# Routing chain of a mixture-of-experts block: fewer steps per first maximum, the last tile's work reordered and partly on GpSimd

## What is computed

```
h = rmsnorm(x, norm2_g) * (1 + sc2) + sh2
g_sel = argmax(h @ w_group + b_group)                 # 1 of 4 groups
e_logits = (h @ w_expert + b_expert)[group g_sel]      # 8 experts of that group
top_v, top_i = top_k(e_logits, 2)
...
xb = rows of h that one expert got, in blocks of 128
ys = (silu(xb @ w1[e]) * (xb @ w3[e])) @ w2[e]
```

## Time and profile before

| what | value |
|---|---|
| median of 3 runs | 2083.99 us (2083.49 to 2084.51) |
| the profiled execution, its own time | 2083.16 us |
| its span on the core | 2080.8 us |
| busy share of the span | PE 96%, PEld 81%, DVE 66%, ACT 46%, POOL 8% |
| chain that ended last | PE 86%, DVE 4%, ACT 4%, issue 2%, DMA 2% |
| last matmul of the output projection begins | 1420.1 us of the span |
| first matmul of the first expert begins | 1447.9 us of the span |

### The profile page before, as it was taken

The page is one execution under the profiler, slowest core; times in us unless marked ns, Lnnn a source line. Parts: engine busy times, 40 slices in busy tenths (PEclk is TensorE's granted clock), DMA queues, the critical chain, the costliest instruction groups (busy, mean ns, idle before and its releaser), DMA issues.

```text
span 2080.8 us, 29320 instructions
## 1 busy us (share of the span) xinstructions
PE 2002.0 (96%) x10099; PEld 1677.0 (81%) x10099; DVE 1366.0 (66%) x2045; ACT 959.8 (46%) x1308; POOL 166.3 (8%) x114
## 2 busy tenths in 40 slices
PE   4999999999999999999999999997999999999995
PEld 4788888888888898888989888886788888888872
DVE  6545443112747658485674745567899999999986
ACT  5211111111453526436263444212888888888863
POOL 0000000000000000000000000000122222222210
PEclk6999999999999999999999999997999999999997
DMA  8142423222212112121120368645999999999955
GB/s 307 46 136 71 141 75 108 71 71 81 49 33 67 53 35 68 40 68 53 35 68 20 96 218 280 202 135 209 340 382 385 382 386 376 383 386 386 399 222 242
DMA packets 209398, 369.69 MB, mean 178 GB/s; under 512 B 43029, under 2 KB 155462, under 8 KB 183750
## 3 DMA queue, kind: packets, MB, share of 16 engines
q1 hardware_dynamic: 190614, 317.63, 43.8%
q10 hardware_dynamic: 9520, 34.63, 4.4%
q0 software_dynamic: 9216, 16.80, 2.1%
HBM read 336.96 MB, written 48.82 MB: 185 GB/s over the span
## 4 chain that ended last, share of the span: by engine, by line
PE 86%; DVE 4%; ACT 4%; issue 2%; DMA 2%; ACTq 1%; SPq 0%; DVEq 0%; POOLq 0%
PE ps L673 41%; PE ps L2581 16%; PE ps L2619 8%; PE ps L2481 4%; PE ps L2381 2%; PE ps L2348 2%; PE ps L2377 1%; PE ps L2567 1%; PE ps L2418 1%; PE ps L2388 1%; PE ps L2432 1%; PE ps L2331 1%; PE ps L2306 1%; PE ps L2603 1%; PE ps L2421 1%
## 5 line engine op out<-in xcount | busy, mean ns | idle before, releaser
L577 DVE TENSOR_TENSOR mw_lo<-mw_raw,mw_hi 128x2048 fp32r<-128x2048 f32 x192 | 436.9, 2289 | 48.9 <-ACT mw_hi L572 48.7
L673 PE MATMUL ps<-h_hi,w_lo 128*128 128x512 f32 x1152 | 463.9, 403 | 3.1 <-DVE h_lo L1453 2.3
L673 PE MATMUL ps<-h_hi,w_hi 128*128 128x512 f32 x1152 | 450.2, 391 | 0.0
L673 PE MATMUL ps<-h_lo,w_hi 128*128 128x512 f32 x1152 | 449.7, 390 | 0.0
L572 ACT ACTIVATE mw_hi<-mw_raw 128x2048 fp32r<-128x2048 f32 x192 | 368.2, 1919 | 117.0 <-PE ps L2581 67.2
L673 PEld LDWEIGHTS ps<-h_hi,w_hi 128*128 128x128 f32 x1152 | 216.9, 188 | 46.2
L673 PEld LDWEIGHTS ps<-h_hi,w_lo 128*128 128x128 f32 x1152 | 217.5, 189 | 43.7 <-issue 2.4
L673 PEld LDWEIGHTS ps<-h_lo,w_hi 128*128 128x128 f32 x1152 | 217.6, 189 | 39.0
L2581 PE MATMUL ps<-mw_hi,xT_lo 128*128 128x512 f32 x512 | 204.1, 399 | 3.3 <-DVE xT_lo L2044 3.1
L2581 PE MATMUL ps<-mw_hi,xT_hi 128*128 128x512 f32 x512 | 201.1, 393 | 0.0
L2581 PE MATMUL ps<-mw_lo,xT_hi 128*128 128x512 f32 x512 | 200.4, 391 | 0.0
(11 more groups left out here) (382 smaller groups left out, 3247.4 us busy)
## 6 DMA issues: line engine op xcount, KB each, us to landing
mw_raw<-in_w_dram SPq DMA_DIRECT2D x192, 1024.0 KB, 7.9
w_raw<-in_w_in_dram SPq DMA_DIRECT2D x72, 512.0 KB, 4.0
ada_b<-in_w_ada_dram SPq DMA_DIRECT2D x8, 2048.0 KB, 8.0
y_t<-y_d SPq DMA_DIRECT2D x8, 1024.0 KB, 10.0
ada_sc<-in_w_ada_dram SPq DMA_DIRECT2D x4, 1024.0 KB, 8.6
w_raw<-in_w_proj_b_dram SPq DMA_DIRECT2D x8, 512.0 KB, 3.6
merged_b_d<-sc_y ACTq DMA_DIRECT2D x8, 512.0 KB, 2.6
gate_a_d<-gate_a ACTq DMA_DIRECT2D x8, 512.0 KB, 2.7
```

The lines of the kernel that those rows point to most:

```text
L577: dve.tensor_tensor(mw_lo[off % NSPLIT][:], mw_raw[off % NRAW][:], mw_hi[off % NSPLIT][:], ALU.subtract).then_inc(mw_lo_done, 1)
L673: last = pe.matmul(dst, lhs[:, s, k], rhs[:, k, cols], start=(k == 0 and part == 0), stop=(k == KD - 1 and part == 2))
```

## The change

1. `first_max` has four steps in place of five. The index tables now count down (`iota_g` 4 to 1, `iota_e` 32 to 1), one scalar_tensor_tensor per tile makes (value == maximum) * index, without a wait between the two tiles, and the first place is a maximum. For the groups the comparison is "not equal", so that the step that subtracted 1 goes.
2. `count(j)` waits for one addition into `e_before`, no longer for two; `pos_one` is made in two halves and `collect(j)` starts on the first. PE's matmul for the totals (L2552 before) comes after `collect(3)`.
3. For the last tile ACT copies the transposed halves before it squares. DVE makes the last tile's reciprocal alone (`new_inv`), and POOL makes its h2 rows in three instructions (`last_h2`).
4. `found_ids` comes ahead of the first weight remainder, writes the ids of the first two experts directly into `tok_now`, and needs no separate cast. The first three remainders follow in a row, then the inputs of the routing weights, the low part of the first rows, and only then `over_counts`, whose prefix sum now runs without copies in zero-padded buffers.

The diff (left out: allocations, constants of step counts, the two index tables, the end of `over_*` where only indices change):

```diff
+            def last_h2(n, s):
+                pool.wait_ge(x1_inv, n + 1)
+                pool.wait_ge(h2_done, n)
+                pool.tensor_scalar(h2_scaled_t[:], x1[:, n], stat2[:, 2, n:n + 1], None, ALU.mult).then_inc(pool_step, 1)
+                pool.wait_ge(pool_step, 10 + len(LEVELS))
+                pool.tensor_tensor(h2_scaled_t[:], h2_scaled_t[:], g2_row[:], ALU.mult).then_inc(pool_step, 1)
+                pool.wait_ge(pool_step, 11 + len(LEVELS))
+                pool.wait_ge(h2_out[s], past(16 * (n // 2)))
+                pool.tensor_tensor(h2[:, s].rearrange("q (k p) -> q p k", p=P),
+                                   h2_scaled_t[:].rearrange("q (p k) -> q p k", p=P),
+                                   sh2_row[:].rearrange("q (p k) -> q p k", p=P), ALU.add).then_inc(h2_done, 1)
+
...
             pool.memset(xg[:], 0.0).then_inc(pool_step, 1)
             pool.wait_ge(pool_step, 9 + len(LEVELS))
+            last_h2(TT - 1, (TT - 1) % 2)
             for n in range(2):
...
+            def turned_x1(n, s):
+                act.wait_ge(logits_done, past(n))
+                for half in range(2):
+                    act.wait_ge(x1_turned, past(2 + 2 * n + half + 1))
+                    act.activation(x1T[s][:, 4 * half:4 * half + 4].rearrange("p k t -> p (k t)"),
+                                   ps[:, 4 + half], ACT.Copy).then_inc(x1T_done, 1)
+
...
             for n in range(TT):
                 s = n % 2
+                if n == TT - 1:
+                    turned_x1(n, s)
...
@@ -1293,12 +1315,8 @@
                 act.wait_ge(x1_squared, n + 1)
                 act.activation(stat2[:, 1, n:n + 1], stat2[:, 0, n:n + 1], ACT.Sqrt, bias=eps_col[:], scale=1.0 / D)\
                    .then_inc(x1_root, 1)
-
-                act.wait_ge(logits_done, past(n))
-                for half in range(2):
-                    act.wait_ge(x1_turned, past(2 + 2 * n + half + 1))
-                    act.activation(x1T[s][:, 4 * half:4 * half + 4].rearrange("p k t -> p (k t)"),
-                                   ps[:, 4 + half], ACT.Copy).then_inc(x1T_done, 1)
+                if n < TT - 1:
+                    turned_x1(n, s)
                 act.wait_ge(h2_done, n + 1)
                 act.dma_start(h2_d[n * P:(n + 1) * P, :], h2[:, s]).then_inc(h2_out[s], 16)
             for off in range(NSPLIT):
...
-            def first_max(one, cand, values, iota, top_):
+            def first_max(one, cand, values, iota, top_, compare=ALU.is_equal):
 
                 n = values.shape[2]
                 link(dve.tensor_reduce(top_, values, AX.X, ALU.max))
-                link(dve.tensor_tensor(cand, values, top_[:, :, None].to_broadcast([P, 2, n]), ALU.is_equal))
-                link(dve.scalar_tensor_tensor(out=cand, in0=cand, scalar=-1000.0,
-                                              in1=iota[:, None, :].to_broadcast([P, 2, n]),
-                                              op0=ALU.mult, op1=ALU.add))
-                link(dve.tensor_reduce(first_at[:], cand, AX.X, ALU.min))
-                link(dve.tensor_tensor(one, cand, first_at[:, :, None].to_broadcast([P, 2, n]), ALU.is_equal))
+                for t in range(2):
+                    ins = dve.scalar_tensor_tensor(out=cand[:, t], in0=values[:, t], scalar=top_[:, t:t + 1],
+                                                   in1=iota[:], op0=ALU.is_equal, op1=ALU.mult)
+                link(ins)
+                link(dve.tensor_reduce(first_at[:], cand, AX.X, ALU.max))
+                link(dve.tensor_tensor(one, cand, first_at[:, :, None].to_broadcast([P, 2, n]), compare))
...
-            def new_h2(n, s):
+            def new_inv(n):
                 col = slice(n, n + 1)
                 dve.wait_ge(x1_root, n + 1)
                 dve.reciprocal(stat2[:, 2, col], stat2[:, 1, col]).then_inc(x1_inv, 1)
                 dve.wait_ge(x1_inv, n + 1)
 
+            def new_h2(n, s):
+                col = slice(n, n + 1)
+                new_inv(n)
                 if n:
...
             def pick_two(j):
 
                 ts = slice(2 * j, 2 * j + 2)
-                first_max(g_one[:], g_cand[:], logits[:, ts, 0:NG], iota_g, best[:, 0, ts])
-                link(dve.tensor_scalar(g_one[:], g_one[:], -1.0, None, ALU.add))
+                first_max(g_one[:], g_cand[:], logits[:, ts, 0:NG], iota_g, best[:, 0, ts], ALU.not_equal)
                 link(dve.scalar_tensor_tensor(
                     out=e_log[:].rearrange("p t (g e) -> p t g e", g=NG),
-                    in0=g_one[:, :, :, None].to_broadcast([P, 2, NG, NE // NG]), scalar=HUGE,
+                    in0=g_one[:, :, :, None].to_broadcast([P, 2, NG, NE // NG]), scalar=-HUGE,
                     in1=logits[:, ts, NG:].rearrange("p t (g e) -> p t g e", g=NG), op0=ALU.mult, op1=ALU.add))
                 first_max(e_one[:, 0, ts], e_cand[:], e_log[:], iota_e, best[:, 1, ts])
                 link(dve.scalar_tensor_tensor(out=e_log[:], in0=e_one[:, 0, ts], scalar=-HUGE, in1=e_log[:],
                                               op0=ALU.mult, op1=ALU.add))
                 first_max(e_one[:, 1, ts], e_cand[:], e_log[:], iota_e, best[:, 2, ts])
                 link(dve.tensor_tensor(e_both[:, ts], e_one[:, 0, ts], e_one[:, 1, ts], ALU.add))
-                for t in range(2 * j, 2 * j + 2):
-                    link(dve.tensor_tensor(e_before[:, t + 1], e_before[:, t], e_both[:, t], ALU.add))
+                link(dve.tensor_tensor(e_before[:, 2 * j + 1], e_before[:, 2 * j], e_both[:, 2 * j], ALU.add))
                 both_step[j] = steps[0]
+                link(dve.tensor_tensor(e_before[:, 2 * j + 2], e_before[:, 2 * j + 1], e_both[:, 2 * j + 1], ALU.add))
                 if j:
...
-                link(dve.tensor_tensor(pos_one[:], iota_p[:, None, :].to_broadcast([P, TOP_K * 2, P]),
-                                       rank[:, j].rearrange("p k t -> p (k t)")[:, :, None]
-                                       .to_broadcast([P, TOP_K * 2, P]), ALU.is_equal))
-                pos_step[j] = steps[0]
+                for k in range(TOP_K):
+                    link(dve.tensor_tensor(pos_one[:, 2 * k:2 * k + 2], iota_p[:, None, :].to_broadcast([P, 2, P]),
+                                           rank[:, j, k, :, None].to_broadcast([P, 2, P]), ALU.is_equal))
+                    pos_step[j, k] = steps[0]
 
             for n in range(TT):
                 new_x1(n, n % 2)
@@ -1931,7 +1951,9 @@
                     tile_logits(n - 1)
                 if n >= 2:
                     (pick_two, place)[n % 2](n // 2 - 1)
-                new_h2(n, n % 2)
+                if n < TT - 1:
+                    new_h2(n, n % 2)
+            new_inv(TT - 1)
             tile_logits(TT - 1)
             pick_two(NP2 - 1)
             place(NP2 - 1)
...
-            def found_ids(dst, found, count, n_done):
+            def found_ids(dst, found, count, n_done, early=False):
                 dve.wait_ge(ids_mm, n_done)
                 link(dve.tensor_scalar(id_far[:, :, 0:count], found, 0.0, far_col[:, 0:1], ALU.is_equal, ALU.mult))
-                link(dve.scalar_tensor_tensor(out=id_f[:, :, 0:count], in0=id_far[:, :, 0:count], scalar=-1.0, in1=found,
+                if early:
+                    dve.scalar_tensor_tensor(out=tok_now[:], in0=id_far[:, 1, 0:2], scalar=-1.0, in1=found[:, 1, 0:2],
+                                             op0=ALU.add, op1=ALU.add).then_inc(tok_ready, 2)
+                link(dve.scalar_tensor_tensor(out=dst, in0=id_far[:, :, 0:count], scalar=-1.0, in1=found,
                                               op0=ALU.add, op1=ALU.add))
-                link(dve.tensor_copy(dst, id_f[:, :, 0:count]))
-
-            split_lo(dve, 0, 0)
-            found_ids(ids[:, :, 0:NE], ps[:, 7, 0:2 * NE].rearrange("p (z b) -> p z b", z=2), NE, NP2)
+
+            found_ids(ids[:, :, 0:NE], ps[:, 7, 0:2 * NE].rearrange("p (z b) -> p z b", z=2), NE, NP2, True)
             dve.sem_inc(ids_ready, 1)
...
-            next_tokens(0, 0, 0)
-            next_tokens(1, 1, 0)
+            for off in range(2):
+                split_lo(dve, 0, off)
+            dve.wait_ge(counts_mm, NP2 + 1)
+            split_lo(dve, 0, 2)
             weight_inputs()
+            turned_lo(0)
             src = over_counts()
             over_total(src)
-            split_lo(dve, 0, 1)
-            turned_lo(0)
-            for off in range(2, 4):
-                split_lo(dve, 0, off)
+            split_lo(dve, 0, 3)
...
             def collect(j):
 
-                pe.wait_ge(r_step, pos_step[j])
                 for v in range(TOP_K * 2):
+                    if v % 2 == 0:
+                        pe.wait_ge(r_step, pos_step[j, v // 2])
                     last = pe.matmul(ps[:, 7, 0:2 * NE].rearrange("p (z b) -> p z b", z=2), pos_one[:, v],
...
             collect(NP2 - 2)
             count(NP2 - 1)
+            collect(NP2 - 1)
```

(1 more changed line is left out.)

34 lines of the change are left out of this document (17 added, 17 removed).

## The result

The changed kernel took **2087.69 us**, the median of 18 runs (2086.42 to 2090.22), against 2083.98 for the kernel before, measured with it in 18 runs (2081.83 to 2088.04). The ratio is 1.0017, with a 95% interval of 1.001 to 1.0023: some 3.7 us slower, inside the 0.2% that was called no change, and 1.4 us above the predicted 2086.3. The profiled execution is the one of 2087.69 us.

The account below looks back on a forecast made before the run. PE is busy nearly throughout, so only its wait before the first expert matmul (1447.90) counts. Savings of 3.25 us against POOL's hold on DVE and a slower gather net 2.35 us later: 2086.3 us, range 2082.0 to 2091.2.

Parts of the forecast that it names:

- Copies ahead of the square: Last tile: PE's route ends near 1426.4 and DVE, free of h2, reads the logits 1.25 us sooner.
- Fewer steps: DVE's last routing: shorter maxima save 0.74 us (0.35 without overlap), count 0.21, an earlier collect some 0.27.
- a pair without a wait between costs little more than one: DVE's maxima: two unlinked steps overlap, as two tok_now copies took 0.21 together; basis of the 0.74 us saving.
- The ids: After collect: no remainder in the way saves 0.18 us, fewer steps to tok_now save 0.60.
- The h2 rows on POOL: Three POOL instructions for the last tile, 1.6, 1.9 and 2.5 us, from 1425.95 to about 1432.2 (1431.3 to 1433).
- Two engines, one way to memory: POOL's h2 work holds DVE's two-input routing steps until 1432.2; ids at 1440.2, 1.4 us later than before.
- The gather: POOL's first gather waits for DVE's first remainder, ends at 1443.5; rows land at 1446.8, 2.35 us later.
- 0.9 before POOL is ready: The last h2 rows' write lands by 1440.4, 0.9 us before POOL could begin the gather, so it costs nothing.
- before 1446: Stated test: if the first expert matmul begins before 1446, the forecast's sign (slower) is wrong.
- POOL starves behind three remainders: Rival: the first gather gets in only after DVE's third remainder; rows 6.8 us later, 2090.8 us; chance 0.25.
- DVE isn't held: Rival: POOL's tensor operations don't stop DVE; ids at 1435.6, total 2081.7 or 2086.1 us by h2 landing; chance 0.18.
- The change pays in full: Rival: no engine holds the other and h2 lands early; 3.25 us sooner, 2080.7 us; chance 0.05.

Follow-up runs that it names:

- e1: The change with its third part undone (last tile's h2 rows on DVE, ACT squares before the copies): ratio 1.0003 to the kernel before, interval 29.03 us.
- e9: e4 with the first rows' low part ahead of remainder 1 and each scalar_tensor_tensor pair replaced by two linked steps: one time, 2083.43 us; interval 26.22.
- e4: The change with h2 rows back on DVE, ACT squaring first, and over_counts again ahead of the remainders: ratio 0.999 to the kernel before, interval 26.68 us.
- e2: The kernel before with only the change's third part (POOL makes the last h2 rows, ACT copies first): ratio 1.0009, interval 30.41 us.
- e5: e4 plus three useless POOL instructions of the form that made h2 rows in the change: one time, 2090.7 us; interval 31.25.
- e7: e5 with all three extra POOL instructions reading one tensor in place of two: one time, 2086.28 us; interval 28.92.
- e8: e1 with the weight loads that the remainders release held until the first gathered rows have landed: one time, 2087.24 us; interval 27.33.
- e10: e4 with the write of the last tile's h2 rows issued only after a later DVE step: one time, 2084.83 us; interval 28.63.

## Why the prediction was right or wrong

The forecast, slower by less than 0.2%, was right; of the interval's 4.37 us its sum had 2.35. It was right by little: the medians lie 3.7 us apart, the line was drawn at 4.2, and the profiles' 4.37 lies beyond it. By its own parts:

1. **Copies ahead of the square** (logits 1.25 sooner): right, 1.20 measured from the mark. `route` began at 1424.52, 0.2 later than put, and the logits were read at 1426.60, 0.2 later than put; e1, with ACT's old order, read them at 1428.06.
2. **Fewer steps** (0.74, or 0.35 if the pairs don't overlap): the steps are gone, but "a pair without a wait between costs little more than one" was wrong, and the size is at its lower end. The pairs take 0.36 to 0.45 and the saving is about 0.36 (0.22 for the group's choice, 0.07 for each expert maximum). The price was read from two copies of 0.15 in the earlier trace rows that overlap by more than half (0.21 for two), and it doesn't carry over to scalar_tensor_tensor: e9. `count` gave 0.23 (0.21 put). `collect` began 0.26 sooner (0.27 put), but the two halves of `pos_one` take 0.88 in place of 0.69, and in e1 and e4, where DVE has the h2 rows behind them, that 0.19 is lost again.
3. **The ids** (0.18 + 0.60): right, if a little high, 0.11 + 0.52. `id_far` follows `collect` after 0.1, and from its start to `tok_now`'s end are 0.55 where there were 1.07 to the first copy.
4. **The h2 rows on POOL** (1.6 + 1.9 + 2.5, to 1432.2): 7.8 with the waits, to 1434.04, beyond the stated 1433. Wrongly sized were the one-input scaling, 2.85 and not 1.6, scaled up from a cast of 128 columns in the earlier trace rows, and the multiplication, 2.40 and not 1.90. The row's operation reads both its operands as broadcasts; whether that is the difference no run shows. The strided write, the one with the wide bounds, was 2.36.

   The Trainium skill (GPSIMD Engine Reference, the cycle accounting) gave 2.25 us for a two-input operation, an estimate from its figure for 2048 columns; the trace has 2.34 to 2.41, so the page was nearer than the row.
5. **Two engines, one way to memory** (DVE held until 1432.2): right in kind, shown by e1, e2 and e5. In size two errors nearly cancelled: POOL ended 1.8 later than put, but its first instruction held nothing, and so the group's choice and the first expert maximum were done before the hold. From POOL's end to the ids 6.2 us passed, put at 8.0. The hold was 3.9 us, put at 4.7 (from 1427.5 to 1432.2), and that the ids came at 1440.27, put at 1440.2, is luck. For the *kind* of POOL instruction the sentence was too general: e7.

   The Trainium skill (SBUF — State Buffer, "Who interferes with whom") calls the port pair that the two engines share an exclusive lock, and has a DVE instruction with two SBUF inputs contend for it with a GpSimd one that reads SBUF. By it the trace agrees for two-input POOL work (2.25, 2.27, 2.39 us) and differs for one-input work (0.22 beside a tensor_scalar of 2.85), so there the measurement decides.
6. **The gather**: here lie the missing 2.0 us. POOL began at 1441.36 (1441.3 put) and was let in after the first remainder, as forecast; it ended 1.1 after it, at 1443.98, and so took 2.62, put at 2.2: 0.4. The sentence that failed is "the rows landed 3.3 after the instruction's end, now at 1446.8". It carried a duration from a place where the last load had been released 3.3 before the instruction's end into one where that is 1.1: **the rows landed 5.06 after, at 1449.04**, the 1.7 of e8. The prediction had said that the loads move, by the remainders' places, but not asked which DMA would then stand first. "0.9 before POOL is ready" was wrong too: the landing time was right (1440.35, put by 1440.4), but POOL needs 1.0 to 1.1 us from the last of its waits to the gather, whichever wait that is; it had been counted for the ids alone. There was no slack (e10). And a first expert matmul "before 1446" was the wrong sign to look for: anything before 1447.9 would have meant faster.

The later events held: DVE was done with the remainders before the transposes needed it (3.41 us idle ahead of `xT_lo`), `over_counts` behind cost nothing (633.0 us from the first expert matmul to the end, 632.9 before), and the gap ahead of the first expert matmul stayed 1.4.

**The rivals.** *POOL starves behind three remainders* fell: POOL's instruction ended after the first and before the second. By the landing alone it would have been taken for true, since its milder form, in after the second, is 4.6 later, the measured 1449.04; only POOL's own row tells them apart. *DVE isn't held* fell on the two steps over 2 us. *The change pays in full* fell with it. What they assumed held for POOL's first instruction alone.

What the change's savings are worth without the h2 rows on POOL: the ids come 1.33 us sooner after the mark in e1 and e4 (17.00, 18.33 before). Of this e4's interval keeps 0.68, since 0.68 is given back where the low part of the rows stands behind remainder 1; e9, with that order mended and two linked steps in place of each pair, keeps 1.14.
